# A first mixer's attention block in another order, without GpSimd, and a sparse loop whose first rounds are reordered

## The chip, the cores and the metric

One core of a Trainium2 chip runs the whole program. Its engines work side by side and meet at semaphores: TensorE (PE in the profile, with PEld for its weight loads) multiplies, VectorE (DVE) and ScalarE (ACT) do the work on elements, GpSimd (POOL) does a little of it, SyncE (SP) issues transfers. The metric is the device time of one execution in microseconds (us), the median over the runs.

## The reference, cut to what matters

The program is three transformer blocks, one after another, on 256 tokens of width 1024, with everything in float32. The change touches two places, both of them attention:

```python
# first block, first mixer
z = x @ w_in[i] + b_in[i]
u_a, v_a, q_b, k_b, v_b, g_a, g_b = jnp.split(z, splits, axis=-1)
...
v = layer_norm(v, ln_g, ln_b)                      # gated branch, 8 groups of 128 columns
s = jnp.einsum('gts,bnsgc->bntgc', w_causal, vc) + b_s.T[None, None, :, :, None]
a = u * s.reshape(bsz, seq, width)
...
o = moba_attention(q_b, k_b, v_b, rel_bias)        # 8 heads of 128; 256 tokens are one
                                                   # causal block: softmax(q k / sqrt(128) + bias) v
m = sigmoid(g_a) * (a @ w_proj_a[i]) + sigmoid(g_b) * (o @ w_proj_b[i])
```

So the first mixer has two branches: a gate (`u` times a mixture of `v` over positions, plus a bias) and an attention of eight heads. The second place is the sparse attention of the second block (NSA): 16 heads of 64, with a compressed branch, a selected branch and a window branch. For 256 tokens the last two are both causal attentions over all tokens, with different keys and values, and their results add up, each scaled by a gate of its own.

## The kernel before, in words

The 256 tokens are two tiles of 128 (`TT = 2`), and 1024 columns are eight blocks of 128 (`DK = 8`). Products are made in parts: ACT copies a weight block's high part (`weights.high`, L366), DVE subtracts it for the low part (`weights.low`, L373), and PE makes three products for each operand pair (`parts_t`, L529 to L531). Weights come by DMA into a ring of four slots of 2 MB. The program is a row of blocks (`nc.Block()`); within one, each engine has its own list of instructions and waits on semaphores, and a block ends for all engines together. The order is written out by hand.

Attention is one class, `Attention`, which works in rounds. A round handles two heads. It has these steps: `scores` (PE, into banks 0 and 1 of the accumulator memory, PSUM, L1087 and L1088 or L2448), `logits` (DVE adds bias or mask and writes to memory, L1092 or L2454), `peaks` (DVE's row maxima, L950), `exponents` (ACT, four of them, each followed by a read of its sum, L958), `normalise` (DVE, a reciprocal L965 and two multiplies L970), `turns` (PE transposes six 128x128 blocks into banks 2 and 3, L977), `keep` (ACT copies them, L1040), and `value_products` (PE, eight products, L985). `products` writes PE's order, `softmax` DVE's, and `tail` ACT's for the loops in which it is used. `self.sooner` rounds have part of their steps placed in earlier blocks (the methods with `sooner` in their name), and `self.turned_sooner` of them are even turned and copied there.

**First mixer.** Four rounds (pairs of heads), `sooner=2`. The block of the input projections ends with four chunks of column products. Before the last chunk PE makes the scores of round 0 (`scores_of(0)`), behind its first block the scores of round 1, both into banks 6 and 7; the second waits until DVE has read the first. DVE splits all 40 weight blocks, then reads the two rounds' scores, and normalises both after ACT's exponentials. ACT evicts PE's results (L1146) and takes the exponentials of round 0 after its 22nd eviction of 24, of round 1 after its 23rd.

The next block is the attention block. PE makes the scores of rounds 2 and 3, turns rounds 0 to 3 and multiplies them, and beside that it mixes the gate's eight groups (L1207), each into half a bank of its own (banks 4 to 7); later the same banks hold the value products. DVE adds the gate's bias for each group (L1235), four at a time behind the peaks of round 2 and of round 3. GpSimd multiplies `uT` by the gate, group by group (L1245). PE waits for all eight bias additions before its first value products, because they overwrite the banks.

**Sparse loop.** Sixteen rounds with `sooner=4`, of which two are turned and copied in the block before the loop: there PE turns round 0, makes sixteen compressed value products (L2725), and turns round 1; ACT copies each (`keep_sooner`, L945). The loop itself stands in `post_norm` (L2290 on) and runs `products`, `softmax` and `tail`. The `fox` mixer behind it uses the same methods with `sooner=2` and `turned_sooner=0`.

## Time and profile before

| what | us |
|---|---|
| median of 3 runs | 3018.94 |
| lowest and highest | 3018.26, 3024.01 |
| profiled execution, its own time | 3021.81 |
| its span | 3020.1 |
| TensorE busy, share | 2904.3, 96% |
| VectorE busy, share | 2287.8, 76% |
| ScalarE busy, share | 1622.2, 54% |
| GpSimd busy, share | 129.9, 4% |
| mean granted clock of TensorE | 0.989 |

Times in the rows below count from the start of the span, in microseconds. A row of a timeline is a run of like instructions merged into one: its start, its length, the engine, the line of the kernel, what it writes and reads, and how many (x8). What stands in brackets behind is how long the engine had been idle before it and what ended that; `PEq` there is PE's sequencer, at the border of two blocks. The granted clock is a share of TensorE's full speed.

### The profile page before, as it was taken

The page shows a single profiled execution, that of the slowest core. Times are in us where ns is not written, and L with a number is a line of the kernel's source. Part 1 is how long each engine was busy: PE and PEld are TensorE (multiplying, and loading weights), DVE is VectorE, ACT ScalarE, POOL GpSimd, SP SyncE. Part 2 cuts the span into 40 slices and gives each one's busy share as a digit, 9 for nine tenths or more (in the row PEclk, how much of TensorE's full clock was granted, in tenths as well). Part 3 has the DMA queues.
Part 4 walks back from the last instruction along what each step waited for, and adds up shares of the span by engine and source line. Part 5 has one row for each costly group of instructions (what it writes and reads, how often), then busy time and mean ns, then how long its engine had stood idle before and what let it go on. Part 6 is the DMA issues. An engine that isn't in the chain of part 4 may idle for free. (4 is left out here: it accounts for less than half of the span.)

```text
span 3020.1 us, 46153 instructions
## 1 busy us (share of the span) xinstructions
PE 2904.3 (96%) x18431; PEld 2477.3 (82%) x18431; DVE 2287.8 (76%) x3619; ACT 1622.2 (54%) x2634; POOL 129.9 (4%) x151
## 2 busy tenths in 40 slices
PE   8899999999999999989999999989999899999998
PEld 7897987778888887857877788768878689999997
DVE  6456699768888887577766777767666788888888
ACT  4444434444444445365454644654355578878876
POOL 0000240000000000200000000000000200000000
PEclk9999999999999999999999999999999899999999
DMA  7454538767777775314544354424553088999895
GB/s 308 150 192 180 222 141 331 296 221 261 273 262 279 287 260 212 143 56 148 186 168 154 112 185 150 163 81 156 188 187 131 17 337 321 334 336 333 319 343 211
DMA packets 81554, 652.10 MB, mean 216 GB/s; under 512 B 6201, under 2 KB 35385, under 8 KB 38993
## 3 DMA queue, kind: packets, MB, share of 16 engines
q1 hardware_dynamic: 50016, 618.47, 54.8%
q10 hardware_dynamic: 31344, 30.93, 3.2%
q8 instruction: 135, 2.21, 0.3%
q14 instruction: 59, 0.48, 0.0%
HBM read 633.66 MB, written 15.73 MB: 215 GB/s over the span
## 5 line engine op out<-in xcount | busy, mean ns | idle before, releaser
L1477 PE MATMUL ps<-x_both,up_hi 128*128 128x512 f32 x1568 | 560.5, 397 | 7.4 <-DVE x_both L797 2.9
L1481 PE MATMUL ps<-x_both,up_lo 128*128 128x256 f32 x1568 | 441.4, 282 | 0.0
L373 DVE TENSOR_TENSOR weight_lo<-ring,weight_hi 128x1024 fp32r<-128x1024 f32 x236 | 287.9, 1229 | 199.4 <-ACT weight_hi L366 198.5
L1477 PEld LDWEIGHTS ps<-x_both,up_hi 128*128 128x128 f32 x1568 | 295.1, 188 | 82.2 <-DVE up_lo L1579 9.5
L366 ACT ACTIVATE weight_hi<-ring 128x1024 fp32r<-128x1024 f32 x236 | 248.1, 1060 | 132.8 <-PE ps L557 55.9
L529 PE MATMUL ps<-x_both,weight_hi 128*128 128x256 f32 x1024 | 292.2, 285 | 10.1 <-DVE x_both L797 3.3
L1481 PEld LDWEIGHTS ps<-x_both,up_lo 128*128 128x128 f32 x1568 | 296.5, 189 | 6.3
L4157 DVE TENSOR_TENSOR up_lo<-ring,up_hi 128x1024 fp32r<-128x1024 f32 x242 | 294.2, 1216 | 0.9 <-ACT up_hi L4306 0.9
L531 PE MATMUL ps<-x_both,weight_lo 128*128 128x256 f32 x1024 | 288.0, 281 | 0.0
L530 PE MATMUL ps<-x_both,weight_hi 128*128 128x256 f32 x1024 | 287.9, 281 | 0.0
L4067 PE MATMUL ps<-up_hi,taken_hi 128*128 128x256 f32 x968 | 285.1, 294 | 1.8 <-DVE hidden_lo L4260 1.8
L1495 PE MATMUL ps<-down_hi,hidden_hi 128*128 128x512 f32 x696 | 274.2, 394 | 1.3 <-DVE hidden_lo L1611 1.2
L4069 PE MATMUL ps<-up_hi,taken_lo 128*128 128x256 f32 x968 | 273.5, 283 | 0.0
L4068 PE MATMUL ps<-up_lo,taken_hi 128*128 128x256 f32 x968 | 273.4, 282 | 0.0
L1499 PE MATMUL ps<-down_lo,hidden_hi 128*128 128x512 f32 x696 | 272.9, 392 | 0.0
L4306 ACT ACTIVATE up_hi<-ring 128x1024 fp32r<-128x1024 f32 x242 | 256.1, 1059 | 22.0 <-PE ps L4069 22.0
L1579 DVE TENSOR_TENSOR up_lo<-ring,up_hi 128x1024 fp32r<-128x1024 f32 (+1 forms) x174 | 235.6, 1355 | 19.2 <-ACT up_hi L1538 19.0
L1584 DVE TENSOR_TENSOR down_lo<-ring,down_hi 128x1024 fp32r<-128x1024 f32 x174 | 212.5, 1221 | 24.1 <-ACT down_hi L1544 23.6
L1544 ACT ACTIVATE down_hi<-ring 128x1024 fp32r<-128x1024 f32 x174 | 183.5, 1055 | 64.1 <-PE ps L1503 64.0
L1503 PE MATMUL ps<-down_hi,hidden_lo 128*128 128x512 f32 x696 | 214.4, 389 | 0.0
L529 PEld LDWEIGHTS ps<-x_both,weight_hi 128*128 128x128 f32 x1024 | 194.7, 190 | 16.5 <-DVE weight_lo L373 6.7
L1538 ACT ACTIVATE up_hi<-ring 128x1024 fp32r<-128x1024 f32 (+1 forms) x174 | 200.7, 1154 | 5.5 <-PEq L2210 4.7
(672 smaller groups left out, 6340.4 us busy)
## 6 DMA issues: line engine op xcount, KB each, us to landing
ring<-in_stream SPq DMA_DIRECT2D x180, 2048.0 KB, 7.8
ring<-in_experts SPq DMA_DIRECT2D x121, 1536.0 KB, 8.5
ring<-in_stream SPq DMA_DIRECT2D x22, 1536.0 KB, 6.3
gates<-kept_gates ACTq DMA_DIRECT2D x14, 1024.0 KB, 8.9
kept_gates<-away_first ACTq DMA_DIRECT2D x8, 896.0 KB, 5.6
kept_gates<-away_last ACTq DMA_DIRECT2D x8, 896.0 KB, 8.1
params_mix<-in_mix SPq DMA_DIRECT2D x1, 3072.0 KB
ring<-in_stream SPq DMA_DIRECT2D x4, 512.0 KB, 7.6
```

What stands on the lines that cost most here:

```text
L373: dve.tensor_tensor(self.place(self.lo, b), self.raw(b), self.place(self.hi, b), ALU.subtract).then_inc(self.split, 1)
L529: first = pe.matmul(out, hi[:, k, :], x_parts[0][:, k, :], start=(n == 0), stop=False)
L530: second = pe.matmul(out, hi[:, k, :], x_parts[1][:, k, :], start=False, stop=False)
L531: last = pe.matmul(out, lo[:, k, :], x_parts[0][:, k, :], start=False, stop=(n == DK - 1))
L1477: last = pe.matmul(out, hi[:, o:o + P], x_both[:, k, :, :].rearrange("p a n -> p (a n)"), start=(n == 0), stop=(n == DK - 1), skip_group_c ...
L1481: last = pe.matmul(out[:, 0:TOKENS], lo[:, o:o + P], x_hi[:, k, :], start=False, stop=(n == DK - 1), skip_group_check=True)
L1495: last = pe.matmul(out, hidden_hi[:, j % 2, tokens], hi[:, o:o + WIDE], start=(starts and i is None and j == 0), stop=False, skip_group_ch ...
L1499: pe.matmul(out, hidden_hi[:, j % 2, tokens], lo[:, o:o + WIDE], start=False, stop=False, skip_group_check=True)
L4067: pe.matmul(to, taken_hi[:, s % 3, k, :], hi, start=(k == 0), stop=False, skip_group_check=True)
L4068: pe.matmul(to, taken_hi[:, s % 3, k, :], lo, start=False, stop=False, skip_group_check=True)
L4069: last = pe.matmul(to, taken_lo[:, s % 3, k, :], hi, start=False, stop=(k == DK - 1), skip_group_check=True)
L4157: dve.tensor_tensor(up_part(up_lo, g, half), raw_up(g, half), up_part(up_hi, g, half), ALU.subtract).then_inc(up_split, 1)
```

## The change

It has these parts.

1. In the input projections' block DVE splits one weight block fewer before it reads the scores of round 0, and the last one between the two rounds. ACT takes both rounds' exponentials one eviction sooner.
2. The attention block's order is written out for each engine instead of coming from `products` and `softmax` with a fill. PE turns round 0 before the scores of round 3, makes the value products of round 0 early, mixes two groups into one bank (`mix_banks`: 6, 7, 0, 1), four matmuls to a signal, and makes the last value products at the end. ACT copies round 0 before the exponentials of round 2. DVE does all softmax steps first, and then for each bank two bias additions and one multiply of 128x512 elements. GpSimd has nothing left.
3. In the block before the sparse loop the second round is turned between the two halves of the compressed value products, and ACT takes the exponential of one column of ones in front of its copies.
4. In the sparse loop (only where rounds were turned sooner) PE makes the scores of round 5 before it turns round 2, and ACT takes the exponentials of round 4 before it copies round 2.

```diff
@@ Attention.products
+                def next_scores(i):
+                    if i > sooner:
+                        pe.wait_ge(self.scores_read, i - sooner)
+                    self.scores(pe, i).then_inc(self.scored, 1)
+                    fill(pe, i)
                 for i in range(sooner - 1, n + 2):
-                    if i + 1 < n:
-                        if i >= sooner:
-                            pe.wait_ge(self.scores_read, i + 1 - sooner)
-                        self.scores(pe, i + 1).then_inc(self.scored, 1)
-                        fill(pe, i + 1)
+                    if i + 1 < n and not (copied and i == sooner):
+                        next_scores(i + 1)
...
+                    if copied and i == sooner - 1:
+                        next_scores(sooner + 1)
@@ Attention.tail
-                    if i >= self.sooner:
+                    if i >= self.sooner and not (i == self.sooner and self.turned_sooner):
                         self.exps(act, i)
+                    if i == self.sooner - 1 and self.turned_sooner:
+                        self.exps(act, i + 1)
@@ mixers, input projections
-                            if at in (3 * DK - 2, 3 * DK - 1):
-                                attend.exps_sooner(act, at - (3 * DK - 2))
+                            if at in (3 * DK - 3, 3 * DK - 2):
+                                attend.exps_sooner(act, at - (3 * DK - 3))
...
-                    weights.low(dve, 40)
                     dve.wait_ge(rel_loaded, 16)
                     for i in range(2):
+                        weights.low(dve, 39 + i)
                         attend.logits_sooner(dve, i, sooner_banks)
@@ mixers, attention block, PE
+                    def scores(i):
+                        if i == 3:
+                            pe.wait_ge(attend.scores_read, 1)
+                        attend.scores(pe, i).then_inc(attend.scored, 1)
+                    def turns(i):
+                        if i >= 1:
+                            pe.wait_ge(attend.turned_copied, i)
+                        if i >= 2:
+                            pe.wait_ge(attend.probs_ready, i - 1)
+                        attend.turns(pe, i).then_inc(attend.probs_turned, 1)
+                    def values_of(i):
+                        pe.wait_ge(attend.turned_copied, i + 1)
+                        if i >= 2:
+                            pe.wait_ge(mixed_read, i - 1)
+                        attend.value_products(pe, i).then_inc(attend.weighted, 1)
+                    def mix(n):
+                        if n == 2:
+                            pe.wait_ge(attend.scores_read, 2)
+                        for g in range(2 * n, 2 * n + 2):
                             for t in range(TT):
...
+                        last.then_inc(mixed, 1)
+                    scores(2)
+                    turns(0)
+                    scores(3)
+                    turns(1)
+                    values_of(0)
+                    mix(0)
+                    mix(1)
+                    turns(2)
+                    values_of(1)
+                    mix(2)
+                    mix(3)
+                    turns(3)
+                    values_of(2)
+                    values_of(3)
@@ ACT
-                    for i in range(2, n_pairs):
-                        attend.exps(act, i)
-                        attend.keep(act, i - 2)
-                    for i in range(n_pairs - 2, n_pairs):
-                        attend.keep(act, i)
+                    attend.keep(act, 0)
+                    attend.exps(act, 2)
+                    attend.keep(act, 1)
+                    attend.exps(act, 3)
+                    attend.keep(act, 2)
+                    attend.keep(act, 3)
@@ DVE, GpSimd
+                    def apply(n):
+                        dve.wait_ge(mixed_read, n + 1)
+                        o = slice(2 * n, 2 * n + 2)
+                        dve.tensor_tensor(uT[:, o, :], uT[:, o, :], gate[:, o, :], ALU.mult).then_inc(gate_ready, 1)
+                    attend.softmax(dve)
+                    for n in range(4):
+                        add(n)
+                        apply(n)
...
-                    for g in range(8):
-                        pool.wait_ge(mixed_read, g + 1)
-                        pool.tensor_tensor(uT[:, g, :], uT[:, g, :], gate[:, g, :], ALU.mult).then_inc(gated, 1)
@@ nsa, block before the loop
                         for b in range(2):
+                            if b == 1:
+                                attend.turn_sooner(pe, 1)
                             for r in range(REP):
...
-                        attend.turn_sooner(pe, 1)
...
+                        act.activation(root_of_one[:], ones[:, 0:1], ACT.Exp)
                         for i in range(2):
                             attend.keep_sooner(act, i)
```

## Rows read from the trace of the kernel before

**Rows 1.** Page, part 1: engine, busy us (share of the span), instructions.

```profile
PE 2904.3 (96%) x18431; PEld 2477.3 (82%) x18431; DVE 2287.8 (76%) x3619; ACT 1622.2 (54%) x2634; POOL 129.9 (4%) x151
```

**Rows 2.** Windows, the attention block: stretch, length, busy us by engine, clock, DMA.

```profile
128.79:148.80 20.01, 15.35 (x104) 13.67 (x105) 9.91 (x20) 6.87 (x21) 6.23 (x8) 1.00 0.00 1
```

**Rows 3.** Timeline, TensorE, 116 to 129: start, us, engine, line, operation, idle before.

```profile
116.17 0.28 PE L531 MATMUL ps<-x_both,weight_lo 128*128 128x256 f32 x1
...
117.11 0.46 PE L1087 MATMUL ps<-kT,qT 128*128 128x128 f32 x2 [0.66 <-DVE prob L1092]
...
126.55 0.28 PE L531 MATMUL ps<-x_both,weight_lo 128*128 128x256 f32 x1
...
128.79 0.46 PE L1087 MATMUL ps<-kT,qT 128*128 128x128 f32 x2 [1.96 <-PEq L1103]
```

**Rows 4.** Timeline, VectorE, 112 to 129.

```profile
114.87 1.23 DVE L373 TENSOR_TENSOR weight_lo<-ring,weight_hi 128x1024 fp32r<-128x1024 f32 x1 [2.56 <-ACT weight_hi L366]
...
116.01 0.95 DVE L1092 SCALAR_TENSOR_TENSOR prob<-ps,params_mix 128x768 f32<-128x768 f32 x1
...
127.44 1.03 DVE L970 TENSOR_TENSOR prob<-prob,total 128x256 f32<-128x256 f32 x2
```

**Rows 5.** Timeline, ScalarE, 112 to 129.

```profile
121.92 1.28 ACT L958 ACT_TABLE_LOAD   x1
...
127.10 0.45 ACT L1146 ACTIVATE kT<-ps,cols 128x256 f32<-128x256 f32 x1
```

**Rows 6.** Timeline, TensorE, 129 to 151.

```profile
130.18 1.95 PE L1207 MATMUL ps<-params_mix,v_a 128*128 128x128 f32 x16
...
131.96 0.82 PE L977 MATMUL ps<-ident,prob 128*128 128x128 f32 x6
...
137.51 1.57 PE L985 MATMUL ps<-hT,v_b 128*128 128x256 f32 x8 [1.64 <-DVE gate L1235]
...
148.80 1.89 PE L597 MATMUL ps<-ones 128*128 128x512 bf16 x8 [0.32 <-PEq L1196]
```

**Rows 7.** Timeline, VectorE, 130 to 141.

```profile
130.38 0.96 DVE L1092 SCALAR_TENSOR_TENSOR prob<-ps,params_mix 128x768 f32<-128x768 f32 x1 [1.91 <-PE ps L1088]
...
132.30 1.41 DVE L1235 TENSOR_TENSOR gate<-ps,params_mix 128x256 f32<-128x256 f32 x4
...
137.58 1.80 DVE L970 TENSOR_TENSOR prob<-prob,total 128x256 f32<-128x256 f32 x2
```

**Rows 8.** Timeline, ScalarE, 132 to 136.

```profile
132.42 0.40 ACT L958 ACTIVATE prob<-prob,top 128x128 f32<-128x128 f32 x1 [4.86 <-DVE top L950]
...
134.19 0.79 ACT L1040 ACTIVATE hT<-ps 128x768 f32<-128x768 f32 x1
```

**Rows 9.** Groups of VectorE by form: busy us, mean ns of one, idle before.

```profile
L3119 DVE TENSOR_TENSOR x<-x,square 128x512 f32<-128x512 f32 x4 | 2.8, 692 | 0.1
...
L512 DVE TENSOR_TENSOR x_both<-uT,x_both 128x256 fp32r<-128x256 f32 x8 | 3.4, 426 | 0.3
```

**Rows 10.** Timeline, TensorE, 1290 to 1303, around the sparse loop's start.

```profile
1290.31 3.72 PE L2725 MATMUL ps<-prob_cmp_t,v_cmp 120*128 120x256 f32 x16
...
1295.84 0.93 PE L2448 MATMUL ps<-qk 64*128 64x128 f32 x8 [1.16 <-PEq L2646]
...
1301.53 0.93 PE L2448 MATMUL ps<-qk 64*128 64x128 f32 x8
```

**Rows 11.** Timeline, ScalarE, 1290 to 1301.

```profile
1294.72 0.81 ACT L945 ACTIVATE prob_t<-ps 128x768 f32<-128x768 f32 x1 [4.29 <-PE ps L977]
...
1299.89 1.28 ACT L958 ACT_TABLE_LOAD   x1
```

**Rows 12.** Timeline, VectorE, 1296 to 1306.

```profile
1303.08 0.18 DVE L965 RECIPROCAL total<-total 128x4 f32<-128x4 f32 x1 [1.15 <-ACT prob L958]
...
1304.43 0.95 DVE L2454 SCALAR_TENSOR_TENSOR prob<-ps,mask 128x768 f32<-128x768 f32 x1
```

**Rows 13.** Windows, 1280 to 1282: the column behind POOL is the granted clock.

```profile
1280.00:1282.00 2.00, 2.00 (x18) 1.76 (x17) 1.63 (x8) 0.37 (x1) 0.00 (x0) 0.50 0.00 0
```

More of the change, by code:

```diff
@@ L1009, in products, with softmax @@
                         self.turns(pe, j).then_inc(self.probs_turned, 1)
-            def softmax(self, dve, between=None):
+            def softmax(self, dve):
                 n, sooner = self.n, self.sooner
@@ L1022, in softmax @@
                         self.peaks(dve, i).then_inc(self.biased, 1)
-                        if between is not None:
-                            between(i)
                     j = i - 1
@@ L1194, in mixers @@
             gate = sbuf("gate", [P, DK, TOKENS], mem=gating)
-            with signals("mixed", "mixed_read", "gated", *Attention.SIGNALS) as (mixed, mixed_read, gated, *sems), nc.Block() as block:
+            with signals("mixed", "mixed_read", "gate_ready", *Attention.SIGNALS) as (mixed, mixed_read, gate_ready, *sems), nc.Block() as block:
                 attend.begin(sems, gating)
+                mix_banks = (6, 7, 0, 1)
                 @block.tensor
                 def _(pe):
-                    def mix(groups):
-                        for g in groups:
-                            if g >= 4:
-                                pe.wait_ge(mixed_read, g - 3)
+                    def scores(i):
[17 more added lines that the diff above has]
+                        for g in range(2 * n, 2 * n + 2):
@@ L1206, in mix @@
                             for t in range(TT):
-                                last = pe.matmul(ps[:, 4 + g % 4, t * P:t * P + P], v_a[:, t, g * P:g * P + P], w_s[:, g, :],
+                                o = g % 2 * TOKENS + t * P
+                                last = pe.matmul(ps[:, mix_banks[n], o:o + P], v_a[:, t, g * P:g * P + P], w_s[:, g, :],
                                                  start=True, stop=True)
-                            last.then_inc(mixed, 1)
-                    def beside(pe, i):
-                        if i == 2:
-                            mix(range(0, 4))
-                        elif i == 3:
-                            mix(range(4, 8))
-                            pe.wait_ge(mixed_read, 8)
@@ L1219, in _ @@
-                    attend.products(pe, beside)
+                        last.then_inc(mixed, 1)
[13 more added lines that the diff above has]
+                    values_of(3)
@@ L1239, in _, with add @@
-                    attend.softmax(dve, between=lambda i: add(range(4 * (i - 2), 4 * (i - 2) + 4)))
-                @block.gpsimd
-                def _(pool):
-                    for g in range(8):
-                        pool.wait_ge(mixed_read, g + 1)
-                        pool.tensor_tensor(uT[:, g, :], uT[:, g, :], gate[:, g, :], ALU.mult).then_inc(gated, 1)
+                    def add(n):
+                        dve.wait_ge(mixed, n + 1)
+                        for g in range(2 * n, 2 * n + 2):
+                            o = g % 2 * TOKENS
+                            last = dve.tensor_tensor(gate[:, g, :].rearrange("p (t n) -> p t n", t=TT),
+                                                     ps[:, mix_banks[n], o:o + TOKENS].rearrange("p (t n) -> p t n", t=TT),
+                                                     spread(b_s[:, g, :], 1, TT), ALU.add)
+                        last.then_inc(mixed_read, 1)
```

6 lines of the change are left out of this document (removed).

## The prediction

> **What bounds the kernel now.** I read the page's head first [rows 1]: TensorE (PE) is busy 96% of a span of 3020.1 us, so a gain can only come from the few places where PE stands still for another engine. Then I read the windows of the stage that the diff rewrites [rows 2]: in its 20.01 us PE is busy 15.35, VectorE (DVE) 9.91, ScalarE (ACT) 6.87, GpSimd 6.23, and no transfer runs. Nothing is full there: the stage is a chain of hand-overs. Last come the timelines, engine by engine, for who is waited for [rows 3 to 9] and the same for the sparse loop [rows 10 to 12]. DMA is idle in the whole stage (share 0.00) because the ring is full, so what is saved in it is not paid back to a transfer right behind it.
>
> Three places stand out.
> (a) End of the input projections. PE ends its last product at 126.83 (126.55 + 0.28) and starts the next block at 128.79 [rows 3]; DVE is what holds the block open, its last normalisation ends at 128.47 [rows 4], 0.32 before PE starts. Earlier PE waits for DVE before the scores of pair 1 (117.11 instead of 116.29, 0.12 behind the product of 116.17), since DVE splits the last weight block (114.87) before it reads the scores of pair 0 (116.01).
> (b) The attention block: PE starts at 128.79 and the block behind it at 148.80, 20.01 us. In each round PE turns probabilities, waits for ACT's copy, and multiplies, one pair after another: the value products begin only at 137.51 [rows 6], though pair 0 and 1 were normalised at the start.
> (c) Sparse loop: the block ends with ACT's copy of the second turned round, 1294.72 + 0.81 = 1295.53, and PE starts at 1295.84 with 1.16 idle [rows 10, 11]. Then DVE cannot normalise round 4 before 1303.08, because ACT first copies, then loads the exponential's table (1299.89, 1.28 us), then takes the exponentials [rows 11, 12].
>
> **Part 1, early rounds (a).** DVE now reads scores 0 before the last split. They are there at about 113.6 (PE has them a round earlier); logits 0.95 and peaks 1.01 end near 115.7, the split of block 39 then ends at about 116.8, and PE needs that block only at about 123.3 (three blocks of about 2.72 us are left, ending at 126.83). So PE goes on at 116.29: 0.82 won. ACT takes the exponentials one eviction sooner: table load 116.97 to 118.25 (1.28 [rows 5]), exponentials of pair 0 until about 120.1, of pair 1 from the next eviction (120.6 to 121.1) until 122.9. DVE normalises until about 124.3, far before the end. The products end at 126.01 and ACT's last eviction (0.45 us, as at 127.10 [rows 5]) at 126.50; the same 0.32 later PE starts the next block: 126.82. **Won: 128.79 - 126.82 = 1.97.** If PE's wait at 117.11 were not DVE's but that of ACT's key column, 0.82 falls away and 1.15 is left; that is the lower bound.
>
> **Part 2, the attention block (b),** from its start as 0. Durations: scores 1.39 from start to next start (128.79 to 130.18), DVE's logits 1.59 behind it and 0.96 long, peaks 1.01, exponentials of a pair 1.77 until ACT's next one (132.42 to 134.19) and 1.86 to the end, a copy 0.80, six turns 0.66 to the next start (131.96, then 132.62), eight value products 1.42 (1.57 whole), four mixing products 0.45 (sixteen take 1.78) [rows 6 to 8].
> PE: scores 2 at 0; turns 0 at 1.39; scores 3 wait for DVE's logits 2 (end 2.55) and start at 2.70; turns 1 at 4.01; values 0 at 4.67; mixing 0 and 1 from 6.09 to 6.99; turns 2 wait for DVE.
> ACT: copy 0 until 3.03; exponentials 2 from 3.63 (peaks end 3.59); copy 1 from 5.40; exponentials 3 from 6.33 to 8.19.
> DVE: logits 3 from 4.29, peaks 3 until 6.29; normalise 2 until 7.47; normalise 3 from 8.23 (exponentials 3) until 9.47. With GpSimd silent I take a normalisation's multiply at 1.03 [rows 4], not the 1.80 that it takes beside GpSimd's multiplies [rows 7].
> PE again: turns 2 at 7.62, values 1 at 8.28, mixing 2 and 3 from 9.70 to 10.60, turns 3 at 10.60, values 2 at 11.26, values 3 at 12.68 (ACT's copy 3 ends at 12.26), end 14.25. So PE no longer waits in the second half.
> DVE's tail, the work taken from GpSimd: per bank two bias additions (0.33 to the next, 0.41 whole: four are 1.41 [rows 7]), a wait for its own result (0.03), and one multiply of 128x512. The kernel before has no such multiply here; the nearest is 0.69 us with both inputs in SBUF [rows 9], about 0.60 until the next instruction. One bank is 0.33 + 0.44 + 0.60 = 1.37, four with a full last one 5.60: from 9.38 to 14.97. The additions for values 2 and 3 are done at 10.1 and 11.5, before PE asks. DVE ends last, PE 0.7 earlier; the next block starts at 14.97 + 0.32 = 15.29. **Won: 20.01 - 15.29 = 4.72.** Bounds of the multiply: below, 0.43 (a 128x256 one, [rows 9]), and then PE's 14.25 decides: 5.4 won; above, 1.80 for a whole 128x768 beside GpSimd gives 1.20 for 512 columns: four times 0.51 more, 2.7 won. I take 0.69 since it has the same shape and operands.
> GpSimd's eight multiplies (6.23 busy) leave. The next block starts with the same ACT and DVE chain; it moves as a whole.
> The Trainium skill (SBUF — State Buffer, SBUF: two separate sides) says that a VectorE instruction with two SBUF inputs and a GpSimd instruction exclude each other for whole instructions. By it the 1.80 goes back to 1.03 and GpSimd's other blocks are untouched; this case's trace agrees, 1.80 against 1.03 [rows 4, 7].
>
> **Part 3, sparse loop (c).** The second turning goes between the two halves of the sixteen compressed value products (3.72 together [rows 10]): PE's work is the same and ends at 1294.68, but ACT's copy now ends near 1293.8, so PE's own end plus 0.30 starts the block: 1294.98, **0.86 won.** From that start as 0: scores 4 at 0, values 0 and 1 at 0.86, scores 5 at 2.31, peaks 4 end 2.97, exponentials 4 from 3.01 to 4.87, DVE normalises round 4 at 5.21 instead of 7.24. But the next thing is late: PE's order now is copy 2 (4.78 to 5.57), values 2 (5.62), turns 3 (6.43), scores 6 (7.23, before 5.69), and logits 6 can start at 8.21 against 8.59 before [rows 12]. So only **0.38** of the two microseconds is kept; behind it DVE's steady period of 3.26 us per round goes on. Sum of part 3: 1.24. Bounds: 0.86 if the loop settles as late as before, and 2.0 if scores 6 were not waited for.
> The added exponential on one column costs its table load, 1.28 [rows 11], and 0.20; ACT is idle from 1287.31 to 1289.63 there, so it is hidden. If that cover were gone, the first copy would be late by up to 1.5, of which 1.7 is free before PE's second turning (1292.1).
> The Trainium skill (ScalarE: Activation LUTs, What ACT_TABLE_LOAD costs) counts 2.66 us for a switch of sets. By it the copy would start 0.5 later and still be in time; the trace shows 1.28 for the load [rows 11] and the first exponential 1.29 behind its start, so here the measurement decides and nothing in the sum hangs on it.
>
> **Sum.** 1.97 + 4.72 + 1.24 = 7.93. The profiled execution took 3021.81 us (span 3020.1); the median of the runs is 3018.94, and they reach from 3018.26 to 3024.01. I subtract from the median: 3011.0.
>
> **The rivals.**
> R1, DVE's tail costs as much as beside GpSimd (multiplies at 1.20, or a wait on its own results far over 0.03), so that the block only wins 2.7: 3018.94 - 5.9 = 3013.0. For it: a chain of twelve DVE instructions ends last. Against it: without GpSimd nothing in the rows slows DVE.
> R2, the reordered sparse loop gives its start back, or ACT's copies hold scores 6 longer: sum 1.97 + 4.72 = 6.7 or less, 3012.2. For it: scores 6 start 1.54 later in their block than before.
> R3, on the other side: PE's clock. Before the sparse loop the granted clock was 0.50 of full speed, 1.2 GHz, in 1280 to 1282, with PE busy all the time [rows 13]. Over the run it was 0.989, which is 33 us of full speed lost, or 66 us at the lower level. Everything behind 127 us moves by seven microseconds against whatever sets these stretches. Each microsecond more at the lower level costs half of one; the change ends slower than before from 16 us more on (a quarter of what there is). Mild forms only blur the gain. Case in full: 3022.
> R4, the edits do nothing for the end: a stage behind is limited by transfers and takes it back, 3018.9. Against it: the DMA share is 0.00 in this stage.
> R5, more: the tail overlaps better and PE's end decides, 5.4 and 2.0: about 3009.
>
> **How the numbers follow.** Forecast 0.64, R1 0.11, R2 0.12, R3 0.04, R4 0.03, R5 0.06. The runs of before differ by 5.8 us among themselves, which is as much as the gain, and 0.2% (6.0 us) is about what a measurement here can tell from no change. The predicted time is the forecast's, 3011.0; the range 3007.5 to 3016.0 holds it with R1, R2 and R5 and half of that spread. Faster by over 0.2% means under 3012.9: most of the forecast's weight, R5 and half of R2, 0.67. Within: R1, R4, the rest, 0.29. Slower 0.04.
>
> **What would show it.** In the profile after: PE's next block starts near 126.8 (part 1); no wait before the scores of pair 1; the block lasts 15.3, with value products of pair 0 near 4.7 and DVE ending last; a 128x512 multiply at 0.69; no GpSimd work in it; normalisations at 1.03; in the sparse part a start 0.3 behind PE's own end, a table load near 1287.3 (before the shift), and a period of 3.26 from round 6 on. The prediction is wrong if PE rests over 1 us in the second half of the attention block, if DVE's tail takes over 7 us, or if the mean clock differs from 0.989 by more than 0.002.

## The result, and the profile after

The changed kernel takes 3025.26 us in the median (3020.64 to 3030.66), the kernel before, beside it, 3020.62 (3017.07 to 3025.86): ratio 1.0016, 95% interval [1.0010, 1.0022]. The forecast was 3011.0. A second measurement of the same kernel, told below, gave 1.0000 [0.9991, 1.0010]. The two intervals meet at 1.0010: no gain where eight microseconds were forecast, and perhaps a small loss. The profiled execution took 3028.96 us. Its head (which answers to [rows 1]):

```profile
span 3027.2 us, 46132 instructions
...
PE 2907.2 (96%) x18410; PEld 2481.3 (82%) x18431; DVE 2290.3 (76%) x3623; ACT 1624.8 (54%) x2635; POOL 124.5 (4%) x143
```

Nothing there gives the place. The waits of the changed kernel between 78 and 102 us, long before the attention block, do (engine and line, what it waited for, us in total, times, longest):

```profile
DVE weight_lo L373 <- DMA params_mix<-in_rel: 10.9, 1, 10.9
...
ACT weight_hi L366 <- PE ps L529: 7.1, 2, 5.5
...
PE ps L529 <- DVE weight_lo L373: 5.4, 1, 5.4
```

These are the instructions, from the timelines of ScalarE's queue, VectorE and TensorE of the changed kernel:

```profile
86.12 0.40 ACTq L1158 DMA_DIRECT2D params_mix<-in_rel  x1
...
92.82 4.63 DVE L373 TENSOR_TENSOR weight_lo<-ring,weight_hi 128x1024 fp32r<-128x1024 f32 x4 [10.94 <-DMA params_mix<-in_rel]
...
94.19 0.55 PE L529 MATMUL ps<-x_both,weight_hi 128*128 128x256 f32 x1 [5.39 <-DVE weight_lo L373]
...
120.52 0.38 PE L1094 MATMUL ps<-kT,qT 128*128 128x128 f32 x2
```

The read is this. ScalarE issues the bias table's transfer at 86.12 and it lands at 92.82, 6.70 later. In the kernel before, `dve.wait_ge(rel_loaded, 16)` stood behind `weights.low(dve, 40)`, so VectorE split on during the transfer, which took 7.9 us there:

```profile
85.15 0.40 ACTq L1151 DMA_DIRECT2D params_mix<-in_rel  x1
...
86.70 1.23 DVE L373 TENSOR_TENSOR weight_lo<-ring,weight_hi 128x1024 fp32r<-128x1024 f32 x1 [1.59 <-ACT weight_hi L366]
89.32 1.23 DVE L373 TENSOR_TENSOR weight_lo<-ring,weight_hi 128x1024 fp32r<-128x1024 f32 x1 [1.40 <-ACT weight_hi L366]
...
112.15 0.38 PE L1087 MATMUL ps<-kT,qT 128*128 128x128 f32 x2
```

In the changed kernel 27 of the 40 splits stand ahead of the wait. The other thirteen, all that were still to do, stand behind it (twelve ahead of the logits of scores 0, one between the two rounds). VectorE stands for 10.94 us, ScalarE for want of TensorE, and TensorE rests 5.39 us. Scores of pair 0 start 34.40 us behind the issue of the transfer; before it was 27.00 (85.15 to 112.15 in the trace of before). I measure from the issue since it cancels what differs in the first 85 us of two executions (what differs behind it stands in experiment 3). The Trainium skill (PSUM — Partial Sum Buffer, Engine vs sequencer instructions) states that VectorE's queue is strictly first in, first out; the trace agrees, four splits whose inputs were ready left in one go only when the transfer had landed.

The clock falls in the rest and stays low behind it. Windows of the changed kernel (stretch, length, busy time and count of TensorE, weight load, VectorE, ScalarE, GpSimd, then the granted clock, DMA share, GB/s):

```profile
88.00:90.00 2.00, 0.80 (x8) 0.60 (x6) 0.00 (x0) 0.47 (x1) 0.00 (x0) 1.00 0.84 350
90.00:92.00 2.00, 0.00 (x0) 0.00 (x0) 0.00 (x0) 0.00 (x0) 0.00 (x0) 0.77 0.79 332
92.00:94.00 2.00, 0.00 (x0) 0.00 (x0) 1.18 (x2) 0.00 (x0) 0.00 (x0) 0.50 0.03 12
94.00:96.00 2.00, 1.81 (x8) 1.84 (x9) 2.00 (x3) 1.06 (x1) 0.00 (x0) 0.50 0.00 0
96.00:98.00 2.00, 2.00 (x12) 2.00 (x11) 1.45 (x2) 0.00 (x0) 0.00 (x0) 0.52 1.04 254
98.00:100.00 2.00, 2.00 (x19) 2.00 (x19) 0.00 (x0) 1.04 (x2) 0.00 (x0) 1.00 0.95 410
```

The clock is at its lower level, 1.2 GHz, from about 91.1 to 97.9. The window at 96 us holds 12 products, the next one, at full clock, 19.

Yet what the change was said to do, it does. The attention block in the changed kernel, windows and then TensorE and VectorE (answers to [rows 2, 6, 7]):

```profile
135.13:150.41 15.28, 14.56 (x104) 13.44 (x105) 11.70 (x24) 6.88 (x21) 0.00 (x0) 1.00 0.00 1
```

```profile
135.13 0.46 PE L1094 MATMUL ps<-kT,qT 128*128 128x128 f32 x2 [0.82 <-PEq L1110]
...
141.10 1.95 PE L1237 MATMUL ps<-params_mix,v_a 128*128 128x128 f32 x16
142.89 0.82 PE L977 MATMUL ps<-ident,prob 128*128 128x128 f32 x6
...
147.30 2.78 PE L985 MATMUL ps<-hT,v_b 128*128 128x256 f32 x16
```

```profile
141.47 1.03 DVE L970 TENSOR_TENSOR prob<-prob,total 128x256 f32<-128x256 f32 x2
143.28 0.18 DVE L965 RECIPROCAL total<-total 128x4 f32<-128x4 f32 x1 [0.79 <-ACT prob L958]
...
148.62 0.75 DVE L1272 TENSOR_TENSOR gate<-ps,params_mix 128x256 f32<-128x256 f32 x2
149.40 0.69 DVE L1281 TENSOR_TENSOR uT<-uT,gate 128x512 f32<-128x512 f32 x1
```

It lasts 15.28 us instead of 20.01, and TensorE is busy 14.56 of it; GpSimd does nothing. (The end at 150.41 is worked out: TensorE's last product ends at 150.08, and 0.33 is the border's rest in experiment 1. The trace has the next block's first record at 150.62, one of eight being missing.) The sparse loop in the changed kernel, TensorE, ScalarE, VectorE (answers to [rows 10, 11, 12]):

```profile
1294.13 1.99 PE L2768 MATMUL ps<-prob_cmp_t,v_cmp 120*128 120x256 f32 x8
...
1298.80 0.93 PE L2489 MATMUL ps<-qk 64*128 64x128 f32 x8 [0.30 <-PEq L2687]
```

```profile
1291.15 1.28 ACT L2798 ACT_TABLE_LOAD   x1
```

```profile
1306.99 0.96 DVE L2495 SCALAR_TENSOR_TENSOR prob<-ps,mask 128x768 f32<-128x768 f32 x1 [1.56 <-PE ps L2489]
```

TensorE rests 0.30 at the border instead of 1.16; from the first compressed product to logits 6 it takes 12.86 instead of 14.12 (1290.31 to 1304.43): 1.26 won.

### The profile page after: what moved, and what is told of

It reads as the page before. It is cut to its first block and busy times, and to the rows that moved or that the text cites. A ratio compares the mean times of both kernels' runs of the same rounds, so it can differ in the third digit from the quotient of the medians.

```text
span 3027.2 us, 46132 instructions
## 1 busy us (share of the span) xinstructions
PE 2907.2 (96%) x18410; PEld 2481.3 (82%) x18431; DVE 2290.3 (76%) x3623; ACT 1624.8 (54%) x2635; POOL 124.5 (4%) x143
```

## The experiments

Differences in microseconds are the ratio's distance from 1 times 3021 unless two medians are named. A half-interval is about 0.9 thousandths, 2.7 us, so single parts of one or two microseconds are read from the traces, and the runs decide on sums.

**1. The wait, put back and moved alone.** Theory: the moved wait costs what the parts win. Rival: the parts lose it elsewhere.

```diff
+                    weights.low(dve, 39)
                     dve.wait_ge(rel_loaded, 16)
```

> The changed kernel with one line more: VectorE splits the weight blocks up to the 39th before it waits for the bias table (the transfer that ScalarE issues in the middle of this block), instead of behind that wait. Theory A (the moved wait is what the change costs: VectorE rests 10.9 us, TensorE 5.4 us and then runs at the lower clock): the attention block starts near 126.8 us instead of 135.1, lasts 15.3, the sparse loop's start is won as in the changed kernel, and the median falls by about 8 us against before, to a ratio near 0.9974. Rival B (the rest of the change costs time too, through later stretches at the lower clock that it brings about): the input projections are mended in the same way, but the median stays within 4 us of before, ratio 0.9987 or more.

Measured: 3016.67 us, ratio 0.9977 [0.9968, 0.9986], 6.9 won. The same kernel once more:

> The same kernel as the first one of this study (all of the change, the wait for the bias table behind the splits), once more, beside the kernels of this call. Theory A (the sparse part wins its 1.24): ratio 0.9974 to 0.9976, below the 0.998 of the kernel without the sparse part. Rival B (the sparse part wins nothing on the whole, as its two halves alone, 1.0007 and 1.0003, and both together, 1.0009, say): ratio 0.9978 to 0.9982.

Measured: 3015.56 us, 0.9976 [0.9967, 0.9985]. One line of order in VectorE's program turns no gain into seven microseconds. In its trace the transfer is issued at 85.62, as late as before, and TensorE has no rest:

```profile
112.61 0.38 PE L1094 MATMUL ps<-kT,qT 128*128 128x128 f32 x2
...
127.22 0.46 PE L1094 MATMUL ps<-kT,qT 128*128 128x128 f32 x2 [0.82 <-PEq L1110]
...
142.50 1.89 PE L597 MATMUL ps<-ones 128*128 128x512 bf16 x8 [0.33 <-PEq L1204]
```

112.61 is 26.99 behind the issue; the attention block starts 14.61 behind it (16.64 before) and lasts 15.28.

The opposite, the wait alone in the kernel before (thirteen splits stand behind it; the eleven in what I expected of this run and of experiment 2, and the nine, are miscounted):

```diff
-                    weights.low(dve, 40)
                     dve.wait_ge(rel_loaded, 16)
+                    weights.low(dve, 40)
```

> The kernel before with one edit: VectorE waits for the bias table before it splits the last eleven weight blocks, all else as before. Theory A: VectorE rests 10.9 us, TensorE about 5.4 us, and the clock falls behind that; the attention block starts some 8 to 9 us later than before (128.8), and the median rises by 8 to 9 us, ratio near 1.0028. Rival C (TensorE's rest alone counts, the lower clock was a chance of that one execution): the attention block starts 5.4 us later, ratio near 1.0018.

Measured: 3030.24 us, 1.0022 [1.0012, 1.0032], between theory A (1.0028) and rival C (1.0018). TensorE rests 5.66 us there, and a stretch at 0.50 of the clock comes with it, from 93.7 to 97.1. It was repeated beside the changed kernel:

> The kernel before with the wait alone moved ahead of the splits, once more. Both theories: the ratio is 1.0018 to 1.0026. Theory A asks that it stands 6 to 8 us above the changed kernel (what the parts win); rival B that it stands 2 to 5 us above it.

> The changed kernel once more, in one call with the wait alone. Theory A (the moved wait costs 7.4 us as in the trace, the rest of the change wins 6 to 7): ratio 1.0001 to 1.0006. Rival B (the wait costs this kernel 10 us or more, since the clock falls behind it): ratio 1.0010 to 1.0020, as in its first runs.

Measured: the wait alone 3029.67 us, 1.0024 [1.0016, 1.0033]; the changed kernel 3021.96 us, 1.0000 [0.9991, 1.0010]. The changed kernel stands 7.7 us below the wait alone, which is the parts' win for a second time, and the wait costs 6.7 to 7.3 by itself. Rival B, that it costs the changed kernel 10 us or more, is not borne out by this measurement: 1.0000 is 7.3 us above the 0.9976 with the wait put back. By the first one, 1.0016, it would be 12. The traces of the changed kernel give 7.4 and 8.2.

**2. The dose.** One, then two of the splits ahead of the wait (28, then 29 in the added line).

```diff
+                    weights.low(dve, 28)
                     dve.wait_ge(rel_loaded, 16)
```

> The changed kernel, with one of the eleven splits put ahead of the wait for the bias table. In the traces so far the transfer lands 6.7 to 8.0 us behind its issue, and TensorE comes to the first block whose split is missing 2.7 us behind the issue; with one split more it comes there at 5.4. Theory A (what the moved wait costs is the time by which the first missing split is late): the rest is 2.7 us instead of 5.4, scores of pair 0 start 30 to 31.5 us behind the issue (27.0 without the wait, 34.4 with it), ratio 0.9985 to 0.9995. Rival B (any rest over a microsecond or two lets the clock fall and costs as much): a stretch at half clock behind the rest, scores at 33 or more, ratio above 1.0005.

> The same with two splits ahead of the wait: TensorE comes to the first missing one at 8.2 us behind the issue, the split ends at 6.9 + 1.2 = 8.1. Theory A: rest under 0.5 us, scores of pair 0 at 27.0 to 27.5 behind the issue, ratio 0.9976 to 0.998, as with the wait put back whole, although VectorE still waits for the transfer ahead of nine splits. Rival B (a late VectorE costs also where TensorE doesn't rest, since the following splits and evictions are pushed together): ratio 0.9985 or higher.

Measured: one split ahead 3021.75 us, 1.0000 [0.9991, 1.0009]; two splits ahead 3018.43 us, 0.9986 [0.9977, 0.9995]. TensorE, first with one and then with two splits ahead, the product that waited and scores 0:

```profile
95.04 0.55 PE L529 MATMUL ps<-x_both,weight_hi 128*128 128x256 f32 x1 [3.60 <-DVE weight_lo L373]
...
119.25 0.39 PE L1094 MATMUL ps<-kT,qT 128*128 128x128 f32 x2
```

```profile
94.94 0.36 PE L529 MATMUL ps<-x_both,weight_hi 128*128 128x256 f32 x1 [1.10 <-DVE weight_lo L373]
...
114.08 0.38 PE L1094 MATMUL ps<-kT,qT 128*128 128x128 f32 x2
```

Set side by side, the issue being at 86.05 and 85.72 in these two, at 85.43 in the changed kernel's repetition, and at 85.81 and 84.95 in the wait alone:

| kernel | TensorE's rest | issue to scores 0 | late by | ratio |
|---|---|---|---|---|
| wait put back | 0 | 26.99 | 0 | 0.9977, 0.9976 |
| two splits ahead | 1.10 | 28.36 | 1.4 | 0.9986 |
| one split ahead | 3.60 | 33.20 | 6.2 | 1.0000 |
| changed kernel | 5.39, 5.27 | 34.40, 35.22 | 7.4, 8.2 | 1.0016, 1.0000 |
| before | 0 | 27.00 | 0 | 1 |
| before, wait alone | 5.66, 5.72 | 34.30, 34.82 | 7.3, 7.8 | 1.0022, 1.0024 |

(Of the 6.2, 0.8 is the effect that experiment 3 tells, not the wait's.) The time follows the lateness, as far as intervals of 2.7 us to either side can tell. Theory A had the order right and missed its figures in both runs. My sizes were too small: the transfer took 7.6 and 7.9 us in these two executions, not 6.9, so one split ahead left 3.60 of rest and not 2.7. With one split ahead a stretch at 0.50 of the clock follows the rest, with two splits none; rival B of the first is right in the stretch and in the lateness (33.20) and wrong in the ratio. In the second, ten splits still wait ahead of the logits. TensorE's rest of 1.10 and 0.3 of the effect told in experiment 3 make up its lateness of 1.4, so the trace shows no further cost; its ratio, 0.9986, is what rival B asked, and its interval reaches theory A's 0.998, so the runs don't decide between them.

**3. Filler in the rest.** 25 products of ones for TensorE ahead of the block it waits with; they compute nothing that is used.

```diff
+                    def filler():
+                        pe.wait_ge(n_read, 4)
+                        keep_warm(pe, 25, 5)
...
+                        if at_t == DK:
+                            after = lambda b: filler() if b == 2 else None
```

> The changed kernel as it is, wait for the bias table included; TensorE gets 25 products of ones (some 0.21 us each, 5.2 us together, into a bank that is read no more) in the place where it rests 5.39 us for the late split. They compute nothing that is used. Theory A (the moved wait costs twice: the rest itself, and then 6.8 us at the lower clock, half of which is lost): the rest and the late scores stay, but no stretch at half clock follows at 90 to 98 us; the scores of pair 0 start some 3.4 us sooner than in the changed kernel (120.5), near 117.2, and the time is 3.4 us below the changed kernel, ratio to the kernel before 1.0005 instead of 1.0016. Rival B (the clock falls there anyway, or the rest alone counts): scores of pair 0 stay near 120.5 and the ratio at 1.0016. Rival C (what is saved at the first stretch comes back as another one in the microseconds behind): no stretch at 90 to 98 but one before 130, time as B.

Measured: 3022.26 us, 1.0009 [1.0000, 1.0018]. Windows of this kernel:

```profile
90.00:92.00 2.00, 2.00 (x11) 0.88 (x9) 0.00 (x0) 0.00 (x0) 0.00 (x0) 1.00 0.28 107
92.00:94.00 2.00, 1.04 (x5) 0.29 (x3) 1.03 (x1) 0.00 (x0) 0.00 (x0) 1.00 0.00 0
94.00:96.00 2.00, 1.66 (x14) 1.69 (x15) 2.00 (x3) 1.06 (x1) 0.00 (x0) 1.00 0.17 41
```

The stretch at the lower clock is gone, so TensorE's rest is what brought it. The price is harder to read. From its restart to scores 0 (nine blocks, 216 products) TensorE takes 25.52 us here (94.34 to 119.86), 26.33 in the changed kernel and 27.27 in its repetition (93.38 to 120.65). But this execution is slow in another way. Windows of it, of the kernel with the border half added (experiment 6) and of the kernel with the wait put back:

```profile
98.00:108.00 10.00, 10.00 (x87) 10.00 (x87) 4.30 (x4) 5.13 (x7) 0.00 (x0) 1.00 0.51 184
```

```profile
98.00:108.00 10.00, 10.00 (x87) 10.00 (x86) 4.23 (x4) 5.20 (x7) 0.00 (x0) 1.00 0.58 211
```

```profile
98.00:108.00 10.00, 10.00 (x91) 10.00 (x90) 4.85 (x4) 4.91 (x8) 0.00 (x0) 1.00 0.58 211
```

All three are at full granted clock with TensorE busy throughout, and the first two make 87 products where the third makes 91: one each 0.118 us instead of 0.113. Such stretches come with and without the moved wait; what sets them is not shown. The last 216 products ahead of scores 0 take 24.48 us with the wait put back (88.13 to 112.61) and 25.44 with the border half (88.83 to 114.27), though neither has a rest or a lower clock there. So the filler's 25.52 holds about 1.0 us of that, and the stretch at the lower clock costs the changed kernel 1.9 and 2.8 us, against the 24.48. For these two it is half of the time in which TensorE worked inside the stretch: 3.72 us (94.19 to 97.91) and 5.71 (93.38 to 99.09). My price of 3.4, half of the whole stretch, was too high, since 3.1 us of the stretch (1.1 in the repetition) had lain in the rest itself, where it costs nothing.

Scores 0 start 34.91 behind the transfer's issue all the same, since the transfer took 8.0 us in this execution, not 6.7, and the products came more slowly: the two cover what the clock gave back. The runs decide nothing either: 1.0009 lies between theory A's 1.0005 and rival B's 1.0016. So the 7.4 and 8.2 us of lateness are, within 0.2, TensorE's rest of 5.4 and 5.3 and the clock's 1.9 and 2.8.

**4. The parts alone.** Part 2, the attention block as the change has it, and nothing else of it:

```diff
-                    attend.products(pe, beside)
+                    scores(2)
+                    turns(0)
+                    scores(3)
...
-                @block.gpsimd
...
+                    for n in range(4):
+                        add(n)
+                        apply(n)
```

> The kernel before with the attention block of the changed kernel alone (its new order, two groups to a bank, the gate's multiply on VectorE). Theory A: the block lasts 15.3 us instead of 20.0, nothing else moves, the median falls by 4.7 us, ratio 0.9984. Rival B: the block is as short, but later stretches at the lower clock take it back, ratio 0.9993 or more.

Measured: 3017.62 us, 0.9985 [0.9976, 0.9994], 4.5 won. Part 1 alone, with the wait behind the splits:

```diff
-                            if at in (3 * DK - 2, 3 * DK - 1):
+                            if at in (3 * DK - 3, 3 * DK - 2):
...
-                    weights.low(dve, 40)
+                    weights.low(dve, 39)
                     dve.wait_ge(rel_loaded, 16)
                     for i in range(2):
+                        weights.low(dve, 39 + i)
```

> The kernel before with part 1 alone: the scores of pair 0 read ahead of the last split, ScalarE's exponentials one eviction sooner, and the wait for the bias table left behind the splits as it was. Theory A (part 1 is worth its rows): the attention block starts 1.97 us sooner against the start of scores 0 (14.67 instead of 16.64), median 2.0 us below the kernel before, ratio 0.9993. Rival B (only the 0.82 of TensorE's wait or the 1.15 of the earlier exponentials is real): 0.8 to 1.2 us below, ratio 0.9996 to 0.9997.

Measured: 3021.04 us, 0.9995 [0.9986, 1.0004]. The interval holds both 2 us and none; the trace tells them apart. Scores 0 start at 112.19, and:

```profile
126.79 0.46 PE L1087 MATMUL ps<-kT,qT 128*128 128x128 f32 x2 [0.82 <-PEq L1103]
```

14.60 instead of 16.64: 2.04. Parts 1 and 2 without part 3 (the kernel with the wait back, the sparse part as before):

> The changed kernel with the wait for the bias table back behind the splits, and with the sparse part as in the kernel before: parts 1 and 2 of the change alone. Theory A (each part is worth its rows: 1.97 and 4.72): median 6.7 us below the kernel before, ratio 0.9978, so 1.2 us above the kernel with part 3 in it (0.9977 in an earlier call, which alone would fit that only within its interval). Rival B (part 3 costs 1 to 2 us that its rows do not show): ratio 0.9972 or lower, below the kernel that has part 3. Against the kernel with the attention block alone (0.9985) either gives the worth of part 1, 2 us.

Measured: 3015.47 us, 0.9980 [0.9970, 0.9989], 6.0 won.

**5. Who ends the attention block?** The last kernel, with VectorE's gate for banks 0 and 1 behind normalise 2 and 3:

```diff
-                    attend.softmax(dve)
+                    for i in range(2, 4):
+                        dve.wait_ge(attend.scored, i - 1)
...
+                        attend.peaks(dve, i).then_inc(attend.biased, 1)
                     for n in range(4):
+                        if n < 2:
+                            dve.wait_ge(attend.exped, n + 1)
+                            attend.normalise(dve, step, n + 2).then_inc(attend.probs_ready, 1)
                         add(n)
                         apply(n)
```

> As the kernel with parts 1 and 2 alone, and VectorE's tail in another order: the bias additions and the multiply of bank 0 directly behind normalise 2, of bank 1 behind normalise 3, then banks 2 and 3. Theory A (VectorE's tail sets the end of the attention block by about 0.7 us, and it rests 0.8 us ahead of normalise 3): the work fills that rest, the block lasts 14.6 us instead of 15.3, and TensorE's own end decides: 0.7 us below the kernel with parts 1 and 2 alone, ratio to the kernel before 0.9976. Rival B (normalise 3 is held up and with it turns 3 and the last two value products): the block lasts 15.5 us or more, and the time is the same or 0.5 us above.

Measured: 3017.06 us, 0.9983 [0.9974, 0.9992], no better. VectorE's last multiply and TensorE's block in this kernel:

```profile
140.40 0.69 DVE L1273 TENSOR_TENSOR uT<-uT,gate 128x512 f32<-128x512 f32 x1
```

```profile
127.02 0.46 PE L1085 MATMUL ps<-kT,qT 128*128 128x128 f32 x2 [0.82 <-PEq L1101]
...
139.19 2.78 PE L985 MATMUL ps<-hT,v_b 128*128 128x256 f32 x16
142.51 0.81 PE L597 MATMUL ps<-ones 128*128 128x512 bf16 x3 [0.54 <-PEq L1195]
```

VectorE ends at 141.09, TensorE at 141.97. From 127.02 to 142.51 it is 15.49, to the hundredth what the kernel without this edit has (126.04 to 141.53). (Both traces lack the record of the first of the eight products of ones behind the block, 0.21, hence 15.49 and not 15.28.) Theory A fell, and rival B too: nothing is held up, TensorE's own work ends the block.

**6. The sparse part.** Both halves in the kernel before, then each by itself: the block ahead of the loop, and the order of the loop's first rounds (TensorE's products and ScalarE's tail):

```diff
                         for b in range(2):
+                            if b == 1:
+                                attend.turn_sooner(pe, 1)
...
-                        attend.turn_sooner(pe, 1)
...
+                        act.activation(root_of_one[:], ones[:, 0:1], ACT.Exp)
```

```diff
+                    if copied and i == sooner - 1:
+                        next_scores(sooner + 1)
...
+                    if i == self.sooner - 1 and self.turned_sooner:
+                        self.exps(act, i + 1)
```

> The kernel before with the parts for the sparse attention alone (second turning between the compressed value products, the early table load, the two first rounds reordered). Theory A: from TensorE's start of the compressed value products to the steady rounds 1.24 us are won (0.86 at the border of the blocks, 0.38 in the first rounds), ratio 0.9996, too small to be told in the times and to be read from the trace. Rival B: the reordered rounds give the start back, the steady rounds come as late as before.

> The kernel before, with only the two edits of the block ahead of the sparse loop: the second turning goes between the halves of the compressed value products, and the exponential on one column loads its table there. Theory A (the two halves of part 3 add up as their rows say): TensorE rests 0.30 us instead of 1.16 at the border, so the profile's loop starts 0.86 sooner; the exponential table is then already loaded at the loop's start. Median 0.9 us below the kernel before, ratio 0.9997. Rival B (this half is what makes the sparse part cost rather than gain, as the run with both halves came out at 1.0009): ratio 1.0005 to 1.0015, with a row that shows TensorE or ScalarE losing more than a microsecond behind the loop. Rival C (the ratio of 1.0009 was the lower-clock stretches' doing): the ratio goes with the mean granted clock, 1 us for each 0.0003 to 0.0005 of it, and no row of the profile gives a loss.

> The kernel before, with only the new order of the loop's first rounds (scores ahead of the turning, exponentials of the next round ahead of the copy). Theory A: the start of the loop stays where it is, at 1.16 us of rest, and logits 6 come 0.4 us sooner behind it than before; median 0.4 us below, ratio 0.9999. Rival B (this half costs): scores 6 are held up by ScalarE's copy and the loop is 1 us or more later from round 6 on, ratio 1.0004 to 1.001. Rival C as for the other half: the ratio follows the granted clock and the profile's rows show no loss.

Measured: both 3023.6 us, 1.0009 [1.0000, 1.0018]; the block ahead of the loop 3024.17 us, 1.0007 [0.9998, 1.0016]; the loop's order 3022.36 us, 1.0003 [0.9994, 1.0012]. And the first half added to parts 1 and 2:

> Parts 1 and 2 with the wait behind the splits, and of the sparse part only the block ahead of the loop (turning between the halves of the products, early table load). Theory A (its row, 0.86 won at the border, stays won): ratio 0.9977, 0.9 us below the kernel with parts 1 and 2 alone (0.998). Rival B (the border's gain goes into more or longer stretches at the lower clock behind it, as its run alone showed a mean clock of 0.9878 against 0.9891): the ratio is 0.998 to 0.9985 and the mean clock of its runs lies below 0.989.

Measured: 3015.45 us, 0.9975 [0.9966, 0.9985], the lowest ratio of all, though not to be told from the kernel with the wait back. From the first compressed product to logits 6 and, seven rounds on, to logits 13, in us: before 14.12 and 36.95; block ahead of the loop alone 12.03 and 34.86; loop's order alone 13.72 and 36.55; both 12.86 and 35.70. VectorE's row for the 12.03 (TensorE's first compressed product is at 1292.84 there):

```profile
1304.87 0.95 DVE L2454 SCALAR_TENSOR_TENSOR prob<-ps,mask 128x768 f32<-128x768 f32 x1
```

So in the trace the early table load and the earlier turning win 2.09 together, more than the 0.86 that I expected of them; the new order of rounds wins 0.40 by itself and loses 0.83 when it is added to the first half.

In the runs none of it can be found. A likely part of the reason lies 300 us further on. Windows, first of the kernel with parts 1 and 2, then of the one with the border half added:

```profile
1592.00:1596.00 4.00, 3.46 (x28) 3.12 (x27) 3.90 (x9) 1.17 (x2) 0.00 (x0) 1.00 0.00 0
1596.00:1600.00 4.00, 4.00 (x36) 4.00 (x36) 2.37 (x3) 1.69 (x4) 0.00 (x0) 1.00 0.30 57
```

```profile
1592.00:1596.00 4.00, 3.46 (x28) 3.13 (x27) 3.90 (x8) 0.86 (x3) 0.00 (x0) 1.00 0.04 12
1596.00:1600.00 4.00, 4.00 (x24) 4.00 (x24) 2.23 (x4) 1.10 (x2) 0.00 (x0) 0.60 0.00 0
```

The rest of 0.54 is the same in both, and only in one does the clock fall behind it, for 3.4 us, of which half, 1.7 us, is lost: 24 products in the window instead of 36. Of the ten profiled executions with the border half, nine have such a stretch between 1590 and 1673 us (seven near 1600, two near 1670); of the eight without it, one. As an estimate from these counts, 1.7 us times the difference of 0.9 and 0.13 is 1.3 us, about as much as the rows say this part wins. That is a count, not a cause; it was not tried apart, and single executions differ by more than this in their other stretches.

## Why the prediction was wrong

The step that failed is in Part 1: "DVE now reads scores 0 before the last split." I read the moved line as one split, block 39, that trades places with the scores' logits. But with `weights.low(dve, 40)` gone from ahead of it, the wait for the bias table stood ahead of all thirteen splits still to do, and I priced neither the wait nor the queue behind it. The rows to price it were there: the transfer's issue in ScalarE's queue at 85.15, and VectorE's splits at 86.70 and 89.32, behind it. The sign that I named for this part, the next block's start near 126.8, came out at 135.13. The shown cost is 6.7 and 7.3 us by itself (experiment 1), and the dose (experiment 2) ties it to the lateness of the first missing split.

The terms of the sum held, each as its rows show it:

- **Part 1**, 1.97 forecast: 2.04 and 2.03 in the traces where the wait is behind the splits. The loss is no part of it: two waits were moved by one edit, and I saw one.
- **Part 2**, 4.72 forecast: 4.73 in the traces, 4.5 in the runs. The normalisation fell from 1.80 to 1.03 and the multiply took 0.69, as said, so R1 is out. One term was mis-sized and hidden: I gave the two banks' mixing 0.90 ("mixing 0 and 1 from 6.09 to 6.99"), and it is 1.79 (141.10 to 142.89). The first row of [rows 6] had it: its sixteen records are four groups of the gate (two records to a product), which is two banks and not four. So TensorE ends at 14.95, not at 14.25, beside VectorE's 14.96, and R5's "PE's end decides, 5.4" could never come. The sum was right by luck, because two ends happened to meet, which experiment 5 showed.
- **Part 3**, 1.24 forecast: 1.26 in the trace. I had the new order of rounds keep 0.38 of what the early exponentials could win. The border's 0.86 came as forecast, and logits 6 start 8.19 behind the loop's start where I had 8.21. What I did not see, the halves show: without the new order the early table load and the earlier turning win 2.09, so on top of them it loses 0.83, though it wins 0.40 by itself. The runs show no gain of this part (1.0009 alone; with and without it 0.9977, 0.9976 and 0.9980). R2 had its place right, the sparse part, and not its mechanism.
- **R3**, the clock: it does fall with the new rest, and its price there is 1.9 to 2.8 us, not the whole loss; half a microsecond for each one at the lower level, as I said, but only where TensorE works. R3 saw later stages as the place and not a new rest. The mean over the runs is 0.9875 after and 0.9891 before, within the 0.002 I named. By estimate these 0.0016 are some 10 us more at the lower level, of which the new stretch is 6.8.
- **The base**: 3018.94 was the median of three runs; over twenty-two it is 3020.62. With it the forecast would have been 3012.7, still out of reach.

Parts 1 to 3 with the wait left behind the splits make 3016.67 and 3015.56 us against 3021.9 and 3022.4. By the ratios that is 6.9 and 7.3 us, where 7.9 was forecast: nearly right, for a kernel that the diff is not.

What stays open: why the sparse part's 1.3 to 2.1 us are missing from the runs, and why the two measurements of the changed kernel stand 1.6 thousandths apart, more than the wait's lateness, 7.4 and 8.2, can give. The mean clock of the two, 0.9875 and 0.9882, accounts by estimate for some 2 of the 4.8 us.

## What to carry to other kernels

When a diff moves a wait on an in-order engine, list every instruction that now stands behind it and wasn't there before, with the time at which each was last needed; a line that looks like the reorder of one step carried thirteen here. Then ask of the awaited transfer when it is issued and how long it takes, from its row in the issuer's queue, not whether it is "long done" where the wait used to be. And when two engines end a stage within a few tenths, work out both ends to the last term before saying which one a further edit must shorten.

## What the runs showed of the hardware

- The same transfer of 1.5 MB took 6.5 to 8.6 us from its issue to the landing in the eighteen profiled executions. Beside the 7.6 the DMA share was 0.94 to 1.09 at 88 to 94 us, beside the 6.6 it was 0.98 and then 0.42 at 88 to 92.
- TensorE's rests of 5.3 to 5.7 us, and one of 3.60, came with a stretch at the lower clock, which began inside the rest or at its end; one of 1.10 did not, nor one of 1.3 behind 5.3 us of filler. Yet behind a rest of 0.54 such a stretch came in one kernel and not in another.
- A stretch at the lower clock costs half of the time in which TensorE works in it: 1.9 and 2.8 us for two of 6.8 us, of which 3.72 and 5.71 were work.
- At a granted clock of 1.00 the same run of products is spaced 0.113 us in some stretches and 0.118 in others, 24.48 against 25.44 us for 216 of them. The cause is not shown.
- Without GpSimd's multiplies a normalisation on VectorE takes 1.03 instead of 1.80 us. The Trainium skill (SBUF — State Buffer, SBUF: two separate sides) says that a VectorE instruction with two inputs in SBUF and a GpSimd instruction that reads SBUF exclude each other for the whole instruction; both traces agree.
